# Moving the modulation vectors from GpSimd products to VectorE multiply-and-sum

## The reference, cut to what matters

```python
c_act = jax.nn.silu(c)                                   # c: 1 x 1024
mod = (c_act @ w_ada + b_ada)[:, None, :]                # w_ada: 1024 x 6144, of each of the 2 layers
sh1, sc1, g1, sh2, sc2, g2 = jnp.split(mod, 6, axis=-1)
h = rms_norm_2(x, norm1_g) * (1 + sc1) + sh1             # then attention, conv, gating
x = x + g1 * (merged @ w_out)
h2 = rms_norm_2(x, norm2_g) * (1 + sc2) + sh2
x = x + g2 * peer_ffn(h2, peer_wq, peer_sub_keys, peer_down, peer_up)
```

## Time and profile before

| | us |
|---|---|
| median of 3 runs | 3586.69 |
| lowest, highest | 3580.44, 3594.11 |
| the profiled execution: its own time | 3591.43 |
| span of that profile | 3590.0 |

### The profile page before, as it was taken

The page is one execution under the profiler, slowest core; times in us unless marked ns, Lnnn a source line. Parts: engine busy times, 40 slices in busy tenths (PEclk is TensorE's granted clock), DMA queues, the critical chain, the costliest instruction groups (busy, mean ns, idle before and its releaser), DMA issues. The chain is left out here.

```text
span 3590.0 us, 48390 instructions
## 1 busy us (share of the span) xinstructions
PE 3048.6 (85%) x18164; PEld 2711.3 (76%) x18164; DVE 2451.5 (68%) x3911; ACT 1484.2 (41%) x2252; POOL 975.7 (27%) x537
## 2 busy tenths in 40 slices
PE   6764799867658998777997999999677987999998
PEld 5664677666546776667987998888667987998887
DVE  5998766569987665446959655665446959555665
ACT  2221453222214432234457444554234457444554
POOL 3355520443555205005960000000006950000000
PEclk9887999988878999778999999999778999999999
DMA  5443444454434444514551566665505641566665
GB/s 206 157 145 136 176 170 145 168 214 145 150 142 170 169 142 167 185 46 153 184 153 48 157 189 184 205 194 169 188 31 166 184 140 48 175 189 185 205 194 162
DMA packets 128232, 568.89 MB, mean 158 GB/s; under 512 B 14155, under 2 KB 24172, under 8 KB 96364
## 3 DMA queue, kind: packets, MB, share of 16 engines
q1 hardware_dynamic: 117916, 505.43, 43.1%
q0 software_dynamic: 9216, 56.63, 4.4%
q10 hardware_dynamic: 864, 3.67, 0.3%
HBM read 551.52 MB, written 15.20 MB: 158 GB/s over the span
## 5 line engine op out<-in xcount | busy, mean ns | idle before, releaser
L1811 PE MATMUL e_ps<-k_hhi,e_hi 128*128 128x256 f32 x2304 | 651.8, 283 | 30.0 <-POOL e_lo L1796 30.0
L1811 PE MATMUL e_ps<-k_hlo,e_hi 128*128 128x256 f32 x2304 | 646.1, 280 | 0.0
L1811 PE MATMUL e_ps<-k_hhi,e_lo 128*128 128x256 f32 x2304 | 644.6, 280 | 0.0
L2069 DVE TENSOR_TENSOR e_lo<-e_raw,e_hi 128x1024 fp32r<-128x1024 f32 x394 | 482.8, 1225 | 203.5 <-ACT e_hi L1893 202.8
L1893 ACT ACTIVATE e_hi<-e_raw 128x1024 fp32r<-128x1024 f32 x544 | 570.9, 1049 | 27.9 <-DMA e_raw<-down 27.0
L721 DVE TENSOR_TENSOR f_wlo<-f_raw,f_whi 128x2048 fp32r<-128x2048 f32 x156 | 392.1, 2529 | 194.1 <-ACT f_whi L539 194.1
L539 ACT ACTIVATE f_whi<-f_raw 128x2048 fp32r<-128x2048 f32 x156 | 296.4, 1912 | 506.8 <-DMA f_raw<-ws 395.7
L1811 PEld LDWEIGHTS e_ps<-k_hhi,e_hi 128*128 128x128 f32 x2304 | 436.6, 189 | 31.7 <-POOL e_lo L1796 31.3
L1811 PEld LDWEIGHTS e_ps<-k_hlo,e_hi 128*128 128x128 f32 x2304 | 436.5, 189 | 0.0
L1811 PEld LDWEIGHTS e_ps<-k_hhi,e_lo 128*128 128x128 f32 x2304 | 436.0, 189 | 0.0
L1796 POOL TENSOR_TENSOR e_lo<-e_raw,e_hi 128x1024 fp32r<-128x1024 f32 x150 | 384.3, 2577 | 89.4 <-ACT e_hi L1893 88.4
(11 more groups left out here) (337 smaller groups left out, 5607.4 us busy)
## 6 DMA issues: line engine op xcount, KB each, us to landing
f_raw<-ws SPq DMA_DIRECT2D x156, 1024.0 KB, 5.0
e_raw<-down SPq DMA_DIRECT2D x288, 512.0 KB, 3.7
e_raw<-up SPq DMA_DIRECT2D x256, 512.0 KB, 3.6
f_x<-ada POOLq DMA_DIRECT2D x48, 1024.0 KB, 5.3
s_raw<-ws SPq DMA_DIRECT2D x24, 1024.0 KB, 5.0
mod_parts<-f_x POOLq DMA_DIRECT2D x48, 128.0 KB, 2.0
s_parts<-mod_parts SPq DMA_DIRECT2D x8, 768.0 KB, 9.5
f_x<-out SPq DMA_DIRECT2D x4, 1024.0 KB, 5.1
```

The lines of the kernel that those rows point to most:

```text
L1811: last = nc.tensor.matmul(psD(n), w, h, start=kt == 0 and i == 0, stop=kt == KT - 1 and i == 2)
L2069: V.tensor_tensor(lo[:, i % RING, :], raw[:, i % RING, :], hi[:, i % RING, :].bitcast(F32), ALU.subtract).then_inc(S["lo_dve"], 1)
```

## The change

The products of the modulation leave POOL. `prepare` spreads `silu(c)` as a row over all partitions and writes it to memory as `c_row` (512 KB). `w_ada` is laid out transposed, 48 tiles of 128 x 1024 for each layer, so that one DVE instruction on a tile, multiply by `c_row` and sum along the row, gives 128 values of the modulation (`accum_out`). The vectors of layer 0 are made in the two passes of `first_layer`, 24 tiles in each, one before every second unit from 28 on; there is one buffer for them. The 48 tiles of layer 1 are made in `peer`, spread over tiles 91 to 264, with two buffers; as `peer` stands in the loop, both of its passes do this, the second to no use. So 144 tiles of 512 KB take the place of 48 loads of 1 MB, 96 of them in `peer`. The loads are in SP's queue ahead of a weight load, with a wait for the buffer in front. `second_mixer` reads the finished columns (two transfers of 12 KB) in place of the parts and the 48 matmuls. SP's loop of `first_layer` is written out.

```diff
+HALF_MOD = 24
+ADA_FROM = 28
+
+
+def ada_tile(u):
+
+    a, r = divmod(u - ADA_FROM, 2)
+    return a if r == 0 and 0 <= a < HALF_MOD else None
...
-    ada = Xr[:, :, :].rearrange("p t n -> p (t n)")
+    ada, c_row = Xr[:, 0, :], Xr[:, 1, :]
...
-                with sp.Fori(1, U1 // NRAW) as i:
-                    for k in range(NRAW):
-                        sp.wait_ge(S["lo_ready"], i * NRAW + (k + 1 - NRAW))
-                        load(i * NRAW + k, k)
-
-                sp.wait_ge(env["out_ada"], l * (16 * ADA_U) + 16 * ADA_U)
+                for u in range(NRAW, U1):
+                    if u == ADA_FROM:
+                        sp.wait_ge(S["x_norm"], NT)
+                        sp.dma_start(c_row, inp["c_row"]).then_inc(S["in_crow"], 16)
+                    a = ada_tile(u)
+                    if a is not None:
+                        if a:
+                            sp.wait_ge(S["ada_done"], a)
+                        sp.dma_start(ada, inp["ada"][bass.ds(l * HALF_MOD + a, 1), :, :].rearrange("o p n -> p (o n)")).then_inc(S["in_ada"], 16)
+                    sp.wait_ge(S["lo_ready"], u + 1 - NRAW)
+                    load(u, u % NRAW)
+
+                sp.wait_ge(S["ada_done"], HALF_MOD)
+                sp.dma_start(inp["mod_cols"][bass.ds(l, 1), :, :].rearrange("o p n -> p (o n)"), MOD).then_inc(S["out_mod"], 16)
                 sp.dma_start(Xr[:, :, :], x_dram).then_inc(S["in_x"], 16)
+                sp.wait_ge(S["out_mod"], 16)
...
-                def modulation(u):
-                    place = inp["ada"][bass.ds(l * ADA_U + u, 1), :, :].rearrange("o p n -> p (o n)")
-                    if u:
-                        pool.wait_ge(env["out_ada"], l * (16 * ADA_U) + u * 16)
-                    pool.dma_start(ada, place).then_inc(env["in_ada"], 16)
-                    pool.wait_ge(env["in_ada"], l * (16 * ADA_U) + (u * 16 + 16))
-                    a3 = ada.rearrange("p (k n) -> p k n", k=KT)
-                    by_c = env["c_act"][:, :].rearrange("p (k n) -> p k n", n=1).to_broadcast([P, KT, 256])
-                    own.link(nc.gpsimd.tensor_tensor(a3, a3, by_c, ALU.mult))
-                    for half in (1024, 512, 256):
-                        own.link(nc.gpsimd.tensor_tensor(ada[:, 0:half], ada[:, 0:half], ada[:, half:2 * half], ALU.add))
-                    parts = inp["mod_parts"][bass.ds(l * ADA_U + u, 1), :, :].rearrange("o p n -> p (o n)")
-                    pool.dma_start(parts, ada[:, 0:256]).then_inc(env["out_ada"], 16)
-
-                for u in range(5):
-                    modulation(u)
...
-                for u in range(5, ADA_U - 4):
-                    modulation(u)
...
-                for u in range(ADA_U - 4, ADA_U):
-                    modulation(u)
...
+                def modulation(u):
+
+                    a = ada_tile(u)
+                    if a is not None:
+                        if a == 0:
+                            dve.wait_ge(S["in_crow"], 16)
+                        dve.wait_ge(S["in_ada"], 16 * (a + 1))
+                        V.scalar_tensor_tensor(ada, ada, 1.0, c_row, ALU.mult, ALU.mult, accum_out=MOD[:, a:a + 1]).then_inc(S["ada_done"], 1)
...
                         converted[0] += 1
+                        modulation(u)
...
+    c_in = pb("p_c", [P, D])
...
+    c_act = pb("p_cact", [P, D])
...
+                act.wait_ge(S["c_ready"], 1)
+                act.dma_start(inp["c_row"], c_act[:, :]).then_inc(S["c_out"], 16)
...
-                quarter = ADA_U // 4
-                for i in range(4):
-                    sp.dma_start(parts[:, i * quarter:(i + 1) * quarter, :],
-                                 inp["mod_parts"][bass.ds(l * ADA_U + i * quarter, quarter), :, :].rearrange("u p n -> p u n")).then_inc(S[f"in_parts{i}"], 16)
+                for half in range(2):
+                    sp.dma_start(mod[:, half * HALF_MOD:(half + 1) * HALF_MOD],
+                                 inp["mod_cols"][bass.ds(l * 2 + half, 1), :, :].rearrange("o p n -> p (o n)")).then_inc(S["in_mod"], 16)
...
-                for c in range(48):
-                    if c % 12 == 0:
-                        pe.wait_ge(S[f"in_parts{c // 12}"], 16)
-                    last = nc.tensor.matmul(psA[:, 3, c:c + 1], parts[:, c // 2, (c % 2) * P:(c % 2 + 1) * P], ones[:, 0:1], start=True, stop=True)
-                last.then_inc(S["mod_mm"], 1)
...
-                dve.wait_ge(S["mod_mm"], 1)
-                own.link(V.scalar_tensor_tensor(mod[:, :], psA[:, 3, 0:48], 256.0, par["b_ada"], ALU.mult, ALU.add))
+                dve.wait_ge(S["in_mod"], 32)
+                own.link(V.tensor_tensor(mod[:, :], mod[:, :], par["b_ada"], ALU.add))
...
+ADA_UNIT = PQ + FIRST + STAGED + 8
+
+
+def next_mod(i):
+
+    k = i - ADA_UNIT
+    a = k * MODS // 176
+    return a if 0 <= a < MODS and (k == 0 or (k - 1) * MODS // 176 < a) else None
...
+                    if i == ADA_UNIT:
+                        sp.wait_ge(S["staged_mult"], 1)
+                        sp.dma_start(c_row[:, :], inp["c_row"]).then_inc(S["in_crow"], 16)
+                    a = next_mod(i)
+                    if a is not None:
+                        if a >= 2:
+                            sp.wait_ge(S["ada_done"], a - 1)
+                        sp.dma_start(ada[a % 2][:, :], inp["ada"][MODS + a, :, :]).then_inc(S["in_ada"], 16)
                     load(i)
...
+                sp.wait_ge(S["ada_done"], MODS)
+                for half in range(2):
+                    sp.dma_start(inp["mod_cols"][2 + half, :, :], modn[:, half * HALF_MOD:(half + 1) * HALF_MOD]).then_inc(S["out_mod"], 16)
+                sp.wait_ge(S["out_mod"], 32)
...
+                def modulation(i):
+
+                    a = next_mod(i)
+                    if a is not None:
+                        if a == 0:
+                            dve.wait_ge(S["in_crow"], 16)
+                        dve.wait_ge(S["in_ada"], 16 * (a + 1))
+                        V.scalar_tensor_tensor(ada[a % 2][:, :], ada[a % 2][:, :], 1.0, c_row[:, :], ALU.mult, ALU.mult,
+                                               accum_out=modn[:, a:a + 1]).then_inc(S["ada_done"], 1)
+
...
                     weigh(n)
                     rest(n + RING)
+                    modulation(n - 2)
...
                     rest(ND + x + RING)
+                    modulation(ND + x - 2)
...
-        for u in range(ADA_U):
-            ada[l * ADA_U + u] = unit_array(w_ada_2[l], 0, 256 * u, "B")
+        ada[l * MODS:(l + 1) * MODS] = w_ada_2[l].T.reshape(MODS, P, D)
```

More of the change, by code:

```diff
@@ L1135, in second_mixer @@
     g1 = pb("s_g1", [P, D])
-    late_at = pb.at[0]
-    parts = pb("s_parts", [P, ADA_U, 256], offset=late_at)
     qn = pb("s_qn", [P, NT, CH])
@@ L1708, in peer @@
     lo = pb("e_lo", [P, RING, D], F32R)
+    modn = pb("e_modn", [P, MODS])
+    B_at = pb.at[0]
     B = pb("e_b", [P, STAGED, T])
@@ L1719, in peer @@
     g_lo = pb("e_glo", [P, 2, T], F32R, offset=hot_at + 4096)
+    c_row = pb("e_crow", [P, D], offset=B_at)
+    ada = [pb("e_ada0", [P, D], offset=B_at + 4096), pb("e_ada1", [P, D], offset=hot_at + 6144)]
     Xr = pb("e_x", [P, NT, D], offset=A_at)
@@ L2240, in second_arrays @@
         pick[bucket[u] if valid[u] else 32, u] = 1.0
-    return dict(c=np.ascontiguousarray(columns(c_2[0])),
+    return dict(c=np.tile(c_2[0], (P, 1)),
                 rel=rel_bias_2, pick=pick, ada=ada, par2=par, ws2=ws2,
@@ L2266 @@
     inp["bias_rows"] = nc.dram_tensor("bias_rows", (P, H2, BIAS_N), F32, kind="Internal").ap()
-    inp["mod_parts"] = nc.dram_tensor("mod_parts", (DEPTH * ADA_U, P, 256), F32, kind="Internal").ap()
+    inp["c_row"] = nc.dram_tensor("c_row", (P, D), F32, kind="Internal").ap()
+    inp["mod_cols"] = nc.dram_tensor("mod_cols", (2 * DEPTH, P, HALF_MOD), F32, kind="Internal").ap()
     inp["out"] = nc.dram_tensor("out", (P, NT, D), F32, kind="ExternalOutput").ap()
```

27 lines of the change are left out of this document (12 added, 15 removed).

## The result

The changed kernel takes 3486.02 us (median of 4 runs, 3483.76 to 3501.01) against 3583.77 for the kernel before on the same chip (4 runs, 3580.44 to 3594.11): a ratio of 0.9731, 95% interval 0.9697 to 0.9766. That is 2.7% faster, 4 us under the forecast of 3490. The profiled execution took 3485.6 us, with a span of 3483.9. The closeness is luck: two terms were far off and their errors cancelled. Most of what follows is about that.

A forecast was written before the change was run, and what follows sets the result against it. DVE, stretched by waiting on POOL, was taken to bound the convolution stretch, and PE to bound `peer`. Terms: -127 - 4 - 2 - 26 + 1.5 + 60 = -97.5 us, giving 3490 us, range 3430 to 3570.

The forecast's parts named there:

- Rival (5): Convolution stretch: something other than POOL stretches the taps, so the gain there falls away; 3617 us, chance 0.04.
- Term A: Convolution stretch of both `first_layer` passes: 127 us less as waiting on POOL goes; bounds 79 and 140.
- rival (3): PE takes over the convolution stretch, packed to 0.75: gain 79 us in place of 127, 3538 us; chance 0.10.
- The price of the new instruction: DVE's multiply-and-sum on a 128 x 1024 tile: 1.35 us, bounds 1.15 and 2.29.
- Rival (1): The summing DVE instruction is slow, 2.41 us in place of 1.35: 3562 us, chance 0.12.
- Term B: Rest of `first_layer`: 4 us less, new tiles otherwise covered; another 2 us less for the final addition.
- Terms C and D: Start of `second_mixer`, 26 us less as the bias table goes out sooner; `prepare`, 1.5 us more for a 512 KB write.
- Term E: `peer`: 60 us more, as weight loads behind new tiles come late for PE; bounds 25 and 138, low end 0.
- case of 7: `peer`: new tile a + 2 stands 7 units after a, 30 of 46; load 5.7 us late, costing 1.0.
- cases of 8: `peer`: new tile a + 2 stands 8 units after a, 16 of 46; load 3.0 us late, costing nothing.
- full margin: `peer`: a weight load may be 4.7 us late before PE waits.
- Rival (2): The added tiles are hidden: `peer` loses 15 us in place of 60, 3445 us; chance 0.17.

The follow-up runs named there:

- The experiment without products: Kernel before without POOL's products and additions, its 48 loads and writes kept, modulation not computed: 3404.24 us, ratio 0.9486.
- `peer` without tiles: Changed kernel without the 48 tiles, sums and `c_row` of `peer`, both mixers taking layer 0's vectors: 3387.26 us, ratio 0.9439 to the kernel before.
- always seven units: Changed kernel, whole, with the 48 tiles of `peer` 3.5 units apart, so tile a + 2 always stands 7 units behind a: 3532.72 us, ratio 0.9856.
- products that nobody reads: Changed kernel with 12 POOL products and their additions in each `first_layer` pass, on an unused tensor without transfers: 3592.94 us, 1.0014 of the kernel before.

## Why the prediction was right, and where it was not

**The reading of the bound: right.** DVE set the tap stretch, and what stretched its instructions was POOL's arithmetic. Both directions were tried: taken away without the transfers it gives the whole gain, and put back without transfers or data it takes 103 of the stretch's 149 us away. The Trainium skill has the mechanism (SBUF — State Buffer, SBUF: two separate sides): VectorE and GpSimd share a pair of ports under an exclusive lock held for a whole instruction, and a VectorE instruction with two SBUF inputs needs it against a GpSimd instruction that reads SBUF. The traces agree: the longest tap of before, 3827 ns, is little over one product's 3.60 us, and goes to 510 when POOL is idle. Rival (5) is dead.

**Term A, -127: it was -149 by the table and -154 from the first tap of all.** The prediction read its windows from 63 and 776 us, where L771 starts. Its first two instructions took 6.0 us from 63.38 us on, where their successors take 0.74 from 64.47 on; the table has them ahead of the stretch. From them to the last tap the stretch took 281.4 and 279.9 us and takes 203.6 in both passes: more was given than the 140 us that the prediction had as its bound. Two steps made the term too small. One is "Between 212 and 221 I take 217". The 221 divided PE's 181 us of busy time by 0.82, as if those 181 us stayed. They were PE's time at a clock of 0.83; at the granted 0.92 of now PE needs 163, and 163 / 0.82 = 199 lies under DVE's floor. DVE stayed the bound, and rival (3), the same thought carried further, was wrong for the same reason. The price of the other engine's work was read at a clock that the change itself moved. The other is the floor itself, 212 and 211 us: the waiting was summed over the taps L774 and the rotation only, and L771 was left out. DVE's groups by form, 63 to 345 us before and 63 to 270 us now:

```profile
L771 DVE TENSOR_SCALAR f_cy<-f_vpad,f_par 128x256 f32<-128x256 f32 x8 | 8.2, 1062 | 1.4 <-PE f_psA L389 1.4
```

```profile
L776 DVE TENSOR_SCALAR f_cy<-f_vpad,f_par 128x256 f32<-128x256 f32 x8 | 2.9, 413 | 1.1 <-PE f_psA L408 1.1
```

That is 5.3 us more of waiting in the first pass. The parts that were summed were right: DVE's busy time on L774 fell by 59.8 us and on the rotation by 13.6.

**The price of the new instruction, 1.35 us: DVE loses 1.14.** The instruction lasts 1.22 and its readout 0.084, but both overlap with their neighbours, and the 0.12 that the prediction added for the readout costs DVE nothing. Rival (1) is dead: the two SBUF sources are fp32, and the instruction runs at 1.19 ns a column. The rule of the Trainium skill that the prediction weighed (Vector Engine (DVE) Microarchitecture Reference, Points that are easy to get wrong), half throughput for such sources, is not borne out against a TENSOR_TENSOR of that size in fp32; the row that it was weighed against was right. No run here has bf16 sources.

**Term B, -4: it was -36** (-34 in the rest of the passes, -2 ahead of the first taps), outside its range of -10 to +10. The cover of the new tiles was right: all 48 cost some 9 us over both passes, 3 to 15 with the scatter, and the 8 on the path alone are 8 x 1.14 = 9. What failed is "I take nothing": the stretched instructions that go were worth far more than nothing. The experiment without products shows it by itself, -18 and -22 us in the rest of the passes. From the last tap to `w_lo` of unit 34, where the layer norm lies, the changed kernel gave 7 us in each pass with the new tile in it; L900 and L901 give the 4.7 predicted. The prediction summed mean less median only over the tap stretch. For the rest of the first pass the trace of before has this row of DVE's groups, 345 to 735 us:

```profile
L721 DVE TENSOR_TENSOR f_wlo<-f_raw,f_whi 128x2048 fp32r<-128x2048 f32 x46 | 121.7, 2663 | 86.1 <-ACT f_whi L539 86.1
```

and that of after, 268 to 647 us:

```profile
L725 DVE TENSOR_TENSOR f_wlo<-f_raw,f_whi 128x2048 fp32r<-128x2048 f32 x46 | 105.3, 2290 | 84.4 <-ACT f_whi L558 84.4
```

That is 46 x (2663 - 2290) = 17 us of waiting on this line alone. A third of it lies in 400 to 600 us, which I had put down as bound by PE, with 192 busy of 200. Half of it, 16 x (2820 - 2290) = 8 us, lies in 600 to 735 us, where PE had 111 of 135: there I had seen that stretched instructions go, and put no price on them.

**Terms C and D, -26 and +1.5: -27.4 and +2.6.** The bias table went out 6.7 us sooner and became what DVE waits for, as written; its landing went from 12.0 to 11.1. DVE starts L1521 16.7 us after the mixer's first load of columns, where L1523 started 29.0 after that of the parts: 17 was written.

**Term E, +60: it was +108, of which the tiles are some 91.** The chain is the one predicted: the sum holds the buffer, SP's queue stands, and the weight load behind it comes late. Moving the sum removes that wait. Its core came out too: the step of PE at a case of 7 is 3.82 us in the mean against 2.78 elsewhere, 1.04 each, and 30 of them give 31 us in a pass. What failed is that the sum counts nothing but these 60 steps, with "In the cases of 8 it is late by 3.0: nothing" and the silent premise that each case starts from the full margin. From tile 91 to the end a pass lost 51 to 53 us. Beside those 31, the unit behind a case of 7 loses 0.2, 6 us; the 16 cases of 8 about 0.2 with their followers, 3; the turn from `down` to `up`, 11.0 us in place of 6.1, 5. Of the 6 to 8 us left, 4.8 are the slower unit of PE, which stands in `peer` without tiles as well. With cases of 8 alone nothing is lost, with cases of 7 alone each costs 1.5 to 1.7: the lateness is carried on. The reason as I read it, which no run isolates: the sum stands behind `lo` of i + 5, and where the tile in between stands at i + 4, that `lo` is itself late by the case before, so the next case is late by more than 5.7. That fits 4.02 and 4.26 against 3.63.

The 1.04 itself is in part luck, for the prediction named the wrong last wait. It had `lo` of DVE as what PE waits for. In `up` PE waits for `g_lo` too. In the kernel before, `lo` ends 2.61 us ahead of its tile's first matmul and `g_lo` only 1.64:

```profile
2403.17 0.42 DVE L2078 TENSOR_TENSOR e_glo<-e_a,e_ghi 128x256 fp32r<-128x256 f32 x1 [0.54 <-ACT e_ghi L1945]
```

In the late cases of 7 of the changed kernel PE starts 0.48 us after the end of `lo` and 0.15 after that of `g_lo`, in nearly every one of 42, and in all 58 of the kernel with always seven units. `g_lo` comes last, because ACT makes `g_hi` behind the late `hi`, and DVE makes `g_lo` behind the late `lo`. So `lo` may slip by 2.61 - 0.48 = 2.1 us and not by 2.7, and the margin of a load in `up` is 4.1 and not 4.7. Against that the load is less late than the 5.7 counted. The sum costs 1.14 in place of 1.35, and behind a new tile a weight load goes out 0.5 us later and lands in 4.4 us in place of 3.6, 1.3 together in place of 1.6. By my estimate 2.72 + 1.14 + 1.3 = 5.2, again about 1 us over the margin.

**Rival (2)** had the better picture of the transfers: they are hidden, and one move of the sum makes it come true: 3394, under its 3445 by what A and B gave more. The total was near 3490 by luck: A and B gave 59 us more, both outside their ranges, and E took 48 more. With 108 for `peer` and the rest as it stood the sum would have been 3538; with `first_layer` as measured and `peer` as it stood, 3431.

**What stays open.** With the sum out of the way `peer` takes 902 us where it took 894 before, and half of its tiles serve nothing, in the second pass. Of those 8 us 4.8 are the slower unit of PE and under 2 the tiles. Why a unit takes 0.03 us longer, in some passes 0.08, with the same work no run shows.

## What to carry to other kernels

Where the mean of an engine's line is well above its median, the difference can belong to another engine, as here: sum it over every line and every stage, not only over the one that the engine bounds, and do not price the engine that comes next from busy time at a clock that the change will move. A load put ahead of a stream in one queue cost next to nothing here once its wait ended before the stream's own wait did; count the steps between the release of the buffer and the next use, look for the last of the waits at that use, and put the releasing instruction as early as its data allow. A margin seems to be spent once: two delays closer together than the queue needs to recover are one chain, so count the whole cycle and not each case against the full margin.

## What the runs showed of the hardware that was not expected

- Products on POOL delayed a stream of short VectorE instructions on SBUF by 0.74 to 0.77 us for each microsecond of POOL's own work, in both kernels that have them; an instruction of 32 columns took 3.05 us beside one.
- `accum_out` on a SCALAR_TENSOR_TENSOR costs nothing in the instruction (1219 ns for 128 x 1024 fp32, where a TENSOR_TENSOR of that size takes 1224 in the mean) and the DVE_READ_ACCUMULATOR of 84 ns behind it overlaps with its neighbours: the next instruction starts 1.14 us after the start of the sum.
- PE's granted clock moved with how much of the tap stretch PE was busy, which other engines set: 0.83 at 181 us busy of 282 before, 0.92 at 166 of 209 with POOL's products gone, 0.84 at 167 of 254 with products that nobody reads, at a like number of matmuls.
- With the transfer engines at 0.74 and 244 GB/s a weight load of 512 KB landed in 3.7 us as before; a load of that size issued beside another took 5.0.
- With the same work and no wait, PE's unit of 24 or 12 matmuls took 2.80 and 2.72 us in the kernel before, and 2.83 and 2.75 in the changed code, with or without the new tiles.
